# Sample tokens leave the dense experts; the recurrence is prepared within the sample attention

## The reference, cut to what matters

```python
xn = rmsnorm(x, norm1_w)
aq, ak, av, hq, hf, hi, hg = split(xn @ w_in)        # 7 pieces of 512
att = dilated_window_attention(aq, ak, av)           # sample tokens also read 2048 cached keys
f = lb + (1 - lb) * sigmoid(hf)
# per token: S = diag(f) S + (1-f) hi^T ; o = S^T silu(hq), evaluated in chunks
o = rmsnorm(hgrn2(silu(hq), 1 - f, hi, log(f), S0)) * silu(hg)
h = x + concat(att, o) @ w_out
# product-key experts: 8 heads, 128 x 128 keys, 16 picks a head = 128 picks a token
e, g = top16_of_pairs(rmsnorm(h, norm2_w) @ wq, sub_keys)   # indices of 16384 experts, softmax weights
y = h + sum_k g_k * gelu(xn2 . u[e_k]) * v[e_k]
y = rmsnorm(y, norm_f_w)
```

## Time and profile before

| | us |
|---|---|
| three runs | 3428.11, 3436.20, 3429.63; median 3429.63 |
| profiled execution | 3433.21, its span 3431.4 |
| PE, DVE, ACT, POOL busy | 94%, 73%, 38%, 30% of the span |
| `expert_inputs` | 1169 to 2339 |
| `expert_outputs` | 2340 to 3431 |
| `attend_sample`, `hgrn` | 498 to 593, 593 to 851 |

### The profile page before, as it was taken

The page is one execution under the profiler, slowest core; times in us unless marked ns, Lnnn a source line. Parts: engine busy times, 40 slices in busy tenths (PEclk is TensorE's granted clock), DMA queues, the critical chain, the costliest instruction groups (busy, mean ns, idle before and its releaser), DMA issues. The chain is left out here.

```text
span 3431.4 us, 54854 instructions
## 1 busy us (share of the span) xinstructions
PE 3219.1 (94%) x20435; PEld 1970.3 (57%) x20435; DVE 2492.2 (73%) x5514; ACT 1311.3 (38%) x2581; POOL 1023.5 (30%) x1076
## 2 busy tenths in 40 slices
PE   7999987698899898999999999996999999999997
PEld 4668652575466554666666666653555555555554
DVE  4222562445423489999999999977988888888887
ACT  3000553321200124677776777743222222222222
POOL 0000000000000003899999999952111111111110
PEclk9999998677999999999999999998999999999998
DMA  3220787422422354878888888899788787787774
GB/s 149 98 98 32 271 297 304 164 88 104 169 65 78 126 186 147 278 276 296 298 295 295 279 284 305 294 348 377 288 293 301 281 305 291 291 297 287 294 289 150
DMA packets 213106, 803.43 MB, mean 234 GB/s; under 512 B 33824, under 2 KB 92320, under 8 KB 169088
## 3 DMA queue, kind: packets, MB, share of 16 engines
q1 hardware_dynamic: 176000, 531.81, 42.5%
q0 software_dynamic: 36864, 268.45, 22.4%
HBM read 665.19 MB, written 201.98 MB: 253 GB/s over the span
## 5 line engine op out<-in xcount | busy, mean ns | idle before, releaser
L1692 PE MATMUL psum<-arena 128*128 128x400 f16 x6144 | 1079.8, 334 | 29.4 <-DVE arena L1740 29.3
L2083 PE MATMUL psum<-arena 128*128 128x400 f16 x6144 | 1048.8, 332 | 25.9 <-DVE arena L2129 25.9
L2083 PEld LDWEIGHTS psum<-arena 128*128 128x128 f16 x6144 | 596.1, 97 | 478.6 <-DVE arena L2129 26.3
L1692 PEld LDWEIGHTS psum<-arena 128*128 128x128 f16 x6144 | 592.6, 98 | 444.7 <-DVE arena L1740 33.6
L1664 POOL TENSOR_SCALAR arena<-arena 128x128 f16<-128x128 f16 x800 | 721.6, 915 | 41.0 <-DVEq L1904 24.2
L116 POOL DMA_INDIRECT arena<-in_experts,arena x256 | 286.3, 1118 | 1131.6 <-DVE arena L149 1040.8
L135 ACT ACTIVATE arena<-arena 128x1 f32<-128x1 f32 x256 | 51.5, 201 | 868.0 <-DVE arena L128 867.7
L149 DVE SCALAR_TENSOR_TENSOR arena<-arena 128x1024 f32<-128x1024 f32 x256 | 331.8, 1296 | 21.3 <-issue 9.6
L2136 DVE TENSOR_TENSOR arena<-arena,psum 128x800 f32<-128x800 f32 x256 | 252.1, 985 | 107.3 <-PE psum L2083 107.3
L128 DVE CUSTOM_DVE_ANT_0 arena<-arena 128x1024 f32<-128x1024 f32 x256 | 312.0, 1220 | 19.0 <-DMA arena<-in_experts,arena 18.0
L1955 ACT ACTIVATE arena<-arena 128x128 f16<-128x128 f16 x800 | 246.0, 388 | 86.9 <-DVE arena L1912 86.2
(11 more groups left out here) (241 smaller groups left out, 3425.0 us busy)
## 6 DMA issues: line engine op xcount, KB each, us to landing
arena<-in_u_feat SPq DMA_DIRECT2D x128, 512.0 KB, 7.0
arena<-in_experts SPq DMA_DIRECT2D x128, 512.0 KB, 5.5
scratch_acts<-arena SPq DMA_DIRECT2D x128, 400.0 KB, 5.3
arena<-scratch_gates SPq DMA_DIRECT2D x32, 1600.0 KB, 8.0
arena<-scratch_acts SPq DMA_DIRECT2D x128, 400.0 KB, 6.6
scratch_gates<-arena SPq DMA_DIRECT2D x48, 1024.0 KB, 8.4
out_k_win_sample<-in_cache_k SPq DMA_DIRECT2D x32, 1022.0 KB, 21.5
out_v_win_sample<-in_cache_v SPq DMA_DIRECT2D x32, 1022.0 KB, 21.3
```

Of the source, the lines that this page charges most:

```text
L1692: last = pe.matmul(psum[:, 2 * p + k, 0:SLD], w[:, s, q, :], xs[:, q, k * SLD:(k + 1) * SLD], start=q == 0 and w is u_hi and xs is x_hi, s ...
L2083: last = pe.matmul(psum[:, 2 * (n % BANKS) + i, 0:SLD], w[:, s, k, q * P:(q + 1) * P], hs[:, s, k, i * SLD:(i + 1) * SLD], start=k == 0 an ...
```

## The change

The sample tile leaves the dense part: `ROWS` becomes 288, `TD` 768, and the products of both expert phases have two pieces of 384 columns. The sample's 32 tokens have 128 picks each; they are laid out as 4 groups of 32 picks by 32 tokens on the 128 partitions, so 32 fetches do them. Their index and weight tables are spread by four small DMAs, the token rows by four more after the last pick of tile 0, and the four partial sums are added by PE at the very end with a matrix of ones (`group_sum`). All 32 are done in `expert_inputs`, behind the 128 of tile 0, and `tick_steps` packs 160 picks into its steps. The sample's units of one-hots and its gates are gone; its search for the greatest pairs stays.

The preparation of the recurrence moves from `hgrn` into `attend_sample` (`center_decays`, `scale_keys`), in place and with the exponential one head at a time. The bias load goes behind the first two key loads.

```diff
-ROWS = 2 * P
+ROWS = 2 * P + NS
 TD = T - ROWS
 SLD = TD // 2
...
+    def index(self, k):
+        part, column = self.plan[k]
+        if part == SAMPLE:
+            return self.m["sample_picks"][:, 0, column:column + 1].bitcast(U32)
+        return self.m["row_index"][:, part, column:column + 1]
...
         if k == 0:
             dve.wait_ge(self.row_loaded, 16)
+        if k == P:
+            dve.wait_ge(self.row_loaded, 16 * (1 + GROUPS_S))
...
 def tick_steps():
-    steps = list(range(9, 21, 2)) + sorted(list(range(20, 120)) + list(range(25, 120, 16))) + [n // 2 for n in range(240, 256)]
-    assert len(steps) == P
+    even = lambda first, last, count: [first + i * (last - first) // count for i in range(count)]
+    steps = list(range(9, 21, 2)) + even(20, 109, P - 6) + even(110, 118, 10) + even(118, PK, NS - 10)
+    assert len(steps) == P + NS and steps == sorted(steps)
...
-    for tile, first in [(TT, 17)] + [(t, 16 * t - 8) for t in range(2, TT)]:
-        rows = NS if tile == TT else P
+    for tile, first in [(t, 16 * t - 8) for t in range(2, TT)]:
+        rows = P
...
             pool.memset(m["row_sums"][:, 0, :], 0.0).then_inc(sums_cleared, 1)
+            pool.memset(m["row_sums"][:, SAMPLE, :], 0.0).then_inc(sums_cleared, 1)
...
+                    elif tile == TT:
+                        dve.tensor_tensor(sample_found[r, 1, :].rearrange("p (h k) -> p h k", h=PH), gate[r], share,
+                                          ALU.mult)
+                        dve.scalar_tensor_tensor(out=picks[r, 2, :], in0=picks[r, 0, :], scalar=float(PK),
+                                                 in1=picks[r, 1, :], op0=ALU.mult, op1=ALU.add)
+                        dve.drain()
+                        dve.tensor_copy(sample_found[r, 0, :].bitcast(U32), picks[r, 2, :])
+                        dve.drain().then_inc(sample_picked, 1)
...
-                at0 = PER * whole + k * NS
-                dve.scalar_tensor_tensor(out=prod[:, e % 2, whole:TD], in0=acts[:, k, whole:TD], scalar=H_SCALE,
-                                         in1=gates[:, g % 2, at0:at0 + NS], op0=ALU.mult, op1=ALU.mult)\
-                   .then_inc(prod_ready, 1)
...
+                if t == TT:
+                    for k in range(2):
+                        last = pe.matmul(psum[0:NS, k, :], group_sum, m["row_sums"][:, SAMPLE, k * 512:(k + 1) * 512],
+                                         start=True, stop=True)
```

In `attend_sample`, DVE's and ACT's lists:

```diff
             normalize(1)
+            center_decays()
+            scale_keys(0)
+            scale_keys(1)
             write_out(0)
+            scale_keys(2)
+            scale_keys(3)
+            dve.wait_ge(rising_ready, 1)
+            dve.tensor_tensor(q, q, f, ALU.mult).then_inc(keys_scaled, 1)
             write_out(1)
...
                 act.activation(silu, silu, ACT.Silu)
-            copy_turned(1)
+            act.wait_ge(decay_dve, 3)
+            for g in range(G):
+                if g >= 1:
+                    act.wait_ge(keys_scaled, g)
+                act.activation(falling, f[:, g, :], ACT.Exp, scale=-1.0).then_inc(falling_ready, 1)
+                if g == 1:
+                    copy_turned(1)
             act.drain()
+            act.activation(f, f, ACT.Exp)
...
+            def center_decays():
+                mid, mid_s = CH // 2 - 1, ST // 2 - 1
...
+                for g in range(G):
+                    dve.tensor_tensor(chunks[:, g], chunks[:, g],
+                                      middle[:, g].unsqueeze(2).broadcast_to([P, NCH, CH]), ALU.subtract)
...
+                dve.tensor_scalar(f, f, 40.0, -40.0, ALU.min, ALU.max)
+                dve.drain().then_inc(decay_dve, 1)
```

In `hgrn` the same work and the waits of PE and SP for it go:

```diff
             load_x(0)
+            sp.dma_start(w_half, x["w_out"][:, 0:4, :]).then_inc(w_half_loaded, 16)
             load_x(1)
...
-            sp.wait_ge(step_dve, 1)
-            sp.dma_start(w_half, x["w_out"][:, 0:4, :]).then_inc(w_half_loaded, 16)
...
-            pe.wait_ge(keys_scaled, 1)
...
-            dve.tensor_tensor(k, k, ek, ALU.mult)
-            dve.drain().then_inc(keys_scaled, 1)
-            dve.wait_ge(step_act, 2)
-            dve.tensor_tensor(q, q, eq, ALU.mult)
```

More of the change, by code:

```diff
@@ L55 @@
 SLOT0 = WORDS - SLOTS * 2 * D
-SUM0 = SLOT0 - 2 * D
+SUM0 = SLOT0 - 3 * D
 XROW0 = SUM0 - D
@@ L99, with __init__ @@
 class Rows:
-    def __init__(self, nc, c, m, x, half, name):
+    def __init__(self, nc, c, m, x, parts, name):
         sem = lambda n: c.enter_context(nc.semaphore(f"{name}_{n}"))
-        self.half, self.table = half, x["experts"]
-        self.slots, self.sums, self.row = m["row_slots"], m["row_sums"], m["x_row"]
-        self.index, self.weight = m["row_index"], m["row_weight"]
+        self.plan = [(part, column) for part in parts for column in range(NS if part == SAMPLE else P)]
+        self.table, self.m = x["experts"], m
+        self.slots, self.row = m["row_slots"], m["x_row"]
         self.dots, self.acts, self.scaled = m["row_dots"], m["row_acts"], m["row_scaled"]
@@ L116, in fetch @@
         pool.indirect_dma_start(out=self.slots[:, k % SLOTS, :], out_offset=None, in_=self.table,
-                                in_offset=bass.IndirectOffsetOnAxis(ap=self.index[:, self.half, k:k + 1], axis=0))\
+                                in_offset=bass.IndirectOffsetOnAxis(ap=self.index(k), axis=0))\
             .then_inc(self.fetched[k % SLOTS], 16)
@@ L139, in scale @@
         act.activation(self.scaled[:, s:s + 1], self.acts[:, s:s + 1], ACT.Copy,
-                       scale=self.weight[:, self.half, k:k + 1]).then_inc(self.scale_ready, 1)
+                       scale=self.weight(k)).then_inc(self.scale_ready, 1)
     def add(self, dve, k):
@@ L834, in _ @@
         def _(dve):
+            dve.memset(sum_state[:, 0], 0.0)
+            dve.drain().then_inc(step_dve, 1)
             dve.wait_ge(loaded, 16 * 5)
[L836 to L857, removed]
-            dve.tensor_tensor(k, k, ek, ALU.mult)
-            dve.drain().then_inc(keys_scaled, 1)
-            dve.wait_ge(step_act, 2)
-            dve.tensor_tensor(q, q, eq, ALU.mult)
-            dve.drain().then_inc(step_dve, 1)
             def copy_out(t):
@@ L983, in attend_sample @@
         lbt = at(word, 8, G); word += 8 * G
+        q, carry, carry_s, falling = feat[:, FHQ, :, :], m["carry"], m["carry_s"], resets
+        middle = at(word, G, NCH); word += G * NCH
+        middle_s = at(word, G, SB); word += G * SB
         assert word <= F0 + 8 * T
@@ L1021, in _ @@
             load_keys(1)
+            sp.dma_start(bias, x["bias_sample"]).then_inc(constants_loaded, 16)
             sp.wait_ge(new_ready, 9)
@@ L1364, in score @@
                         last = pe.matmul(psum[0:rows, 6 + (p + b) % 2, (t % 4) * P:(t % 4 + 1) * P],
-                                         query[:, p, t * P:t * P + rows],
+                                         query[:, p, column(t):column(t) + rows],
                                          arena[:, bass.ds(word_keys + i * 2 * PK + p * PK, PK)],
@@ L1492 @@
 TOP_STEPS = piece_steps()
-TURN_STEPS = [None, 15] + [first - 2 for first in (24, 40, 56, 72, 88, 104)] + [None]
+TURN_STEPS = [None, None] + [first - 2 for first in (24, 40, 56, 72, 88, 104)] + [None]
 HALF = P // 2
@@ L1528, in expert_inputs @@
     before_tile = {u["tile"]: u["group"] for u in reversed(UNITS)}
-    order = {tile: j for j, tile in enumerate([TT] + list(range(2, TT)))}
-    before_last = {tile: before_tile.get(tile - 1 if 2 < tile < TT else TT, 0) for tile in order}
+    order = {tile: j for j, tile in enumerate(range(2, TT))}
+    before_last = {tile: before_tile.get(tile - 1, 0) for tile in order}
+    last_of_rows = max(n for n, ticks in enumerate(TICKS) if P - 1 in ticks)
     STORES = 4
@@ L1624, in _ @@
                         load_scores(j)
+                if n == TOP_STEPS[1][-1] + 1:
+                    sp.wait_ge(sample_picked, 1)
+                    for j in range(GROUPS_S):
+                        sp.dma_start(m["sample_picks"][j * NS:(j + 1) * NS],
+                                     sample_found[0:NS, :, j * NS:(j + 1) * NS]).then_inc(sample_spread, 16)
+                if n == last_of_rows + 1:
+                    sp.wait_ge(rows_of.dot_ready, P)
+                    for j in range(GROUPS_S):
+                        sp.dma_start(rows_of.row[j * NS:(j + 1) * NS, :], x["normed"][SAMPLE][0:NS, :])\
+                          .then_inc(rows_of.row_loaded, 16)
                 sp.wait_ge(gelu_done, n + 1)
@@ L1883, in copy_picks @@
             def copy_picks(tile):
-                rows = NS if tile == TT else P
-                r = slice(0, rows)
+                r = slice(0, P)
                 dve.wait_ge(picks_turned, order[tile] + 1)
@@ L2067, in _ @@
             pool.memset(y_sum, 0.0).then_inc(cleared, 1)
+            pool.tensor_tensor(group_sum, m["ident"][:, 0:NS], m["ident"][:, NS:2 * NS], ALU.add).then_inc(cleared, 1)
+            for j in range(2, GROUPS_S):
```

(2 more changed lines are left out.)

130 lines of the change are left out of this document (81 added, 49 removed).

## The result

The changed kernel took **3457.64 us** (median of five, 3450.74 to 3461.47) against 3429.16 for the kernel before in the same session: a ratio of 1.0079, 95% interval 1.0063 to 1.0094. It is 28 us slower, outside the 0.3% that counts as no change; the forecast was 3435, with 0.41 on slower. The profiled execution took 3461.47, span 3459.6, so the spans differ by 28.2 as well.

A forecast was written before the change was run, and what follows sets the result against it. PE and DVE were both taken as full in the expert inputs, PE alone as the bound in the outputs. Terms -27.1 -1.5 -41.4 +61.8 +14 +0.3 sum to +6.1: 3435 us on the median's scale, range 3396 to 3470.

The forecast's parts named there:

- Recurrence preparation and sample attention (-27.1 and -1.5): Recurrence starts earlier with its preparation hidden in the sample attention, -27.1 us; bias load behind two key loads, -1.5.
- rival 3: Recurrence: the preparation does not fit in the sample attention and the recurrence starts no earlier; 3462 us, chance 0.05.
- Expert outputs (-41.4): Expert outputs: 6144 matmuls each lose 16 of 400 columns, -41.0 us, and DVE's small sample product goes, -0.4.
- Picks on DVE (28 x 2.54 = +71.1): Expert inputs up to step 118: 28 extra picks cost DVE a dot and an add, 2.54 us each, +71.1.
- DVE's waits in that stretch still near zero.: Middle of the expert inputs: a sign that the forecast is right, DVE waiting for almost nothing there.
- the upper middle of +33 to +75: Expert inputs up to step 118: +61.8 us chosen between bounds +33 (gaps take picks) and +75 (dear adds, late rows).
- rival 2: Expert inputs: rows come late behind GpSimd's one-hots, DVE waits 1.2 us in each of 35 steps; +42, 3477, chance 0.18.
- The last ten steps (+14): Expert inputs from step 118: four more row fetches on full DMA engines, 10.5 us, plus 3.5; bounds 4 and 20.
- The 3.5 us for the three-pick steps: Steps 118 and 123 of the expert inputs: some fetches are released only in the step that wants them, +3.5 us.
- The rule that spoke against the change: Expert inputs: two-SBUF-input VectorE instructions and SBUF-reading GpSimd ones exclude each other, so added dots and adds hold up POOL.
- Rival 1: Expert inputs: DVE's 28 us of gaps absorb picks and the tail hides; 3400 us, chance 0.17 (0.03 for its extreme).

The follow-up runs named there:

- e2: The changed kernel, but the 32 sample picks are taken in the expert outputs and the inputs keep the old 128 picks; 3351.25 us, 0.9761 to before.
- e3: The changed kernel, but PE turns a tile's picks in the seventh part of its product, not the second; 3458.98 us, 1.0075 to before.
- e5: The changed kernel, but every fifth pick's dot and add in the expert inputs cover 32 columns, not 1024; 3411.95 us, 0.9948 to before.
- e9: The changed kernel with the same 160 picks, six of them taken in other steps; 3448.28 us, 1.0047 to before.
- e1: The kernel before with only the sample attention and recurrence changes, experts as before; 3404.06 us, 0.9910 to before.
- e4: The changed kernel, but GpSimd makes the first one-hots of every second token only, the other gates left out; 3411.81 us, 0.9941 to before.
- e8: e2 with two of each unit's eight first one-hots made by ScalarE, plus eight late picks moved to the outputs; 3343.10 us, 0.9748 to before.

## Why the prediction came out as it did

**Recurrence preparation and sample attention (-27.1 and -1.5).** Right. PE's transposes start 28.5 us earlier, the updates 28.8; DVE's second key product ends at 565.7 (forecast 567.1) and the query product at 583.2 (584.5). The whole first stretch gained 27.0. In e2, e3 and e5 to e9, which share its code up to there, it took 1136.1 to 1144.3 us, so a microsecond or two of it tell nothing. e1 gives -28.0 alone; rival 3 is out.

**Expert outputs (-41.4).** Right: -40.0, 6.5 ns a matmul.

**Picks on DVE (28 x 2.54 = +71.1).** Right in sum, and partly by luck: over 64 steps of the middle the change took 644.8 us for 88 picks and the kernel before 581.2 for 68. Less 12.0 us of waits that is 2.58 us for each of the 20. The groups of the kernel before in its 64 steps, against those of the change shown at e4:

```profile
L1912 DVE TENSOR_SCALAR arena<-arena 128x128 f16<-128x128 f16 x512 | 146.8, 373 | 0.5
L149 DVE SCALAR_TENSOR_TENSOR arena<-arena 128x1024 f32<-128x1024 f32 x68 | 89.9, 1322 | 9.6 <-issue 5.7
...
L128 DVE CUSTOM_DVE_ANT_0 arena<-arena 128x1024 f32<-128x1024 f32 x68 | 82.4, 1216 | 0.0
```

Adds and dots grew by 24.3 and 22.4 us, 2.3 us for each of the 20 picks. Another 8.1 us is DVE's own one-hots, as many as before but 398 ns in place of 373: a term that the sum put at nothing.

**"DVE's waits in that stretch still near zero."** This step failed, and with it the choice of the upper middle of +33 to +75: the stretch took +75.1. The working against rival 2 was an average: eight one-hots at 612 ns and 4.5 us of two-input work are 9.4, under a step of 9.8. But the work is not spread evenly: of sixteen units of a tile one or two meet DVE's longest instructions and take over 10 us, and three of the two-pick steps (36, 52 and 68, with 14.8 of the 16.9 us) stood right behind two such units. Rival 2 happened in that form: not 1.2 us in each of 35 steps (42 us), but 5 waits with 16.9 us in the middle; 3.6 us less of the other terms stand against it. The trace before showed the spread, 590 to 3704 ns, and I used the median.

**The last ten steps (+14).** Right in kind, small in size: +20.1, my upper bound. The 3.5 us for the three-pick steps were the mis-sized term: step 118 alone waited 9.16 us, again behind eight one-hots. e4 and e9 each take 10.7 us off this stretch, e9 with two picks fewer in it.

**The rule that spoke against the change.** GpSimd's one-hots are longer beside DVE's wide instructions (10.80 against 4.66 us), and DVE's own are shorter with fewer of GpSimd's (e4, 398 to 340 ns). Both agree with the Trainium skill (SBUF — State Buffer, Who interferes with whom), by which VectorE and GpSimd contend for a pair of SBUF ports that they share. Its part on tensor_scalar, which in a two-port mode can also take that pair, is the one that fits DVE's one-hots, a tensor_scalar with one tensor; I had weighed only instructions with two SBUF inputs. That the mode is the cause was not tried.

**Rival 1** is out: steps were 10.08 us in the middle. The sum of the measured terms, -27.0 +75.1 +20.1 -40.0, is the 28.2 us found.

## What to carry to other kernels

Work put on an engine that is full cost its whole price there, and the freed time of its partner was lost: e2 and the change compute the same, and putting the picks where DVE still waited for PE was worth 106 us. Read an engine's room from its waits for others, in the very stretch where the work is to stand, not from its missing busy time (e8). Where a queue mixes transfers with work of uneven length, check the longest stretch ahead of each transfer, not the mean.

## What the runs showed of the hardware

VectorE's 128x128 f16 one-hots are stretched by what GpSimd does beside them, though VectorE's own instructions are the same: 398 ns in the change, 367 to 373 with as many of GpSimd's but one pick a step, 340 with half of GpSimd's. In e4's trace 128 of them ran while GpSimd did nothing, 305 ns on the mean. GpSimd's fetches stretch them too: in the change 68 stood beside the issue of an indirect DMA and no one-hot of GpSimd, 427 ns on the mean, though 30 such in e4 took only 326.

After a pause of PE the granted clock was lower. PE waited 4.00 us in step 38, and the next 24 matmuls took 5.75 us, 240 ns each, where one of the same form takes 164 in the outputs (timeline, PE; then two stretches as above, before and after the wait):

```profile
1493.89 0.55 PE L1755 MATMUL psum<-consts,arena 128*128 128x128 f32 x3 [4.00 <-DVEq L1932]
1494.27 5.75 PE L1742 MATMUL psum<-arena 128*128 128x384 f16 x24
```

```profile
1486.80:1489.90 3.10, 3.09 (x21) 1.67 (x18) 3.02 (x11) 2.46 (x8) 3.10 (x5) 1.00 0.95 386
1493.90:1500.10 6.20, 6.20 (x32) 3.50 (x33) 5.83 (x8) 1.45 (x3) 4.52 (x4) 0.72 0.95 326
```

The granted clock was 1.00 of 2.4 GHz before the wait and 0.72 on the mean of the 6.2 us after it, so part of these ran at the lower level, 1.2 GHz. Over the whole middle it was 0.97 against 1.00 before. As PE was not the bound, it cost nothing here: e3 moved these pauses and gained nothing.
